# Sparse attention planned by beats: another order of the tiles, an earlier start of attending, and fewer filler products

## The reference, cut to what matters

```python
scores = indexer_scores(iqb, iwb, ik)                      # sum over 8 heads of w * relu(q_idx . k_idx)
scores = jnp.where((key_pos[None, :] <= qpos[:, None])[None], scores, -jnp.inf)
_, idx = lax.top_k(scores, n_sel)                          # n_sel = 256
valid = idx <= qpos[None, :, None]
return selected_attention(qb, gather_rows(k, idx), gather_rows(v, idx), valid)
```

## Time and profile before

| | us |
|---|---|
| median of three executions | 7112.57 |
| lowest and highest | 7103.77, 7126.53 |
| profiled execution, own time | 7120.96 |
| its span, first to last instruction | 7118.9 |

### The profile page before, as it was taken

The page is one execution under the profiler, slowest core; times in us unless marked ns, Lnnn a source line. Parts: engine busy times, 40 slices in busy tenths (PEclk is TensorE's granted clock), DMA queues, the critical chain, the costliest instruction groups (busy, mean ns, idle before and its releaser), DMA issues. The chain is left out here.

```text
span 7118.9 us, 108460 instructions
## 1 busy us (share of the span) xinstructions
PE 6246.8 (88%) x36876; PEld 3865.7 (54%) x36876; DVE 4227.9 (59%) x9694; ACT 4048.7 (57%) x5650; POOL 1652.2 (23%) x4028
## 2 busy tenths in 40 slices
PE   6999998878999999999999989797999599999960
PEld 2888886223454444444444455574555366767640
DVE  1555554478888888888888987553666510111027
ACT  1555554578898889999998888322333121222125
POOL 0111110222212322222332222001111133333335
PEclk9999998689999999999999999888999699999985
DMA  6121111000000000000000000332333388888888
GB/s 216 43 42 49 46 44 33 7 4 5 5 6 6 7 7 9 9 9 9 9 9 8 8 7 7 127 119 84 106 103 100 130 338 320 335 337 334 315 300 305
DMA packets 283509, 703.77 MB, mean 99 GB/s; under 512 B 105461, under 2 KB 151541, under 8 KB 242324
## 3 DMA queue, kind: packets, MB, share of 16 engines
q0 software_dynamic: 69408, 432.04, 16.3%
q1 hardware_dynamic: 210464, 252.99, 10.8%
q10 hardware_dynamic: 3190, 13.05, 0.5%
HBM read 559.38 MB, written 138.74 MB: 98 GB/s over the span
## 5 line engine op out<-in xcount | busy, mean ns | idle before, releaser
L1088 DVE TENSOR_SCALAR_CACHE_REDUCE at_junk<-at_key,at_thr 128x320 int8<-128x320 int16 (+44 forms) x990 | 1436.0, 1452 | 146.1 <-POOL at_thr L853 119.8
L887 ACT ACTIVATE at_junk<-at_key,at_thr 128x64 int8<-128x64 f32 (+47 forms) x627 | 1048.4, 1672 | 111.4 <-POOL at_thr L853 96.5
L1146 DVE CUSTOM_DVE_ANT_0 at_sm<-at_pS,at_drop 128x512 f32<-128x512 f32 (+3 forms) x1152 | 723.5, 642 | 176.8 <-PE at_pS L975 174.7
L975 PE MATMUL at_pS<-keep_KT,at_q 64*128 64x512 f32 (+3 forms) x2304 | 619.5, 615 | 82.5 <-DVE at_mx L1146 80.2
L1006 PEld LDWEIGHTS at_pT<-keep_ident,at_sm 128*128 128x128 f32 x4224 | 468.2, 144 | 410.2 <-issue 381.0
L986 PE MATMUL at_pD<-keep_IKT,at_iq 32*128 32x512 f32 (+3 forms) x2272 | 649.4, 649 | 17.9 <-ACT at_relu L911 17.0
L936 ACT ACTIVATE at_pt_sb<-at_pT 128x1024 f32<-128x1024 f32 (+2 forms) x576 | 548.8, 953 | 181.7 <-PE at_pT L1006 180.3
L911 ACT ACTIVATE at_relu<-at_pD 128x1024 f32<-128x1024 f32 (+3 forms) x568 | 542.2, 955 | 175.5 <-PE at_pD L986 172.9
L1006 PE MATMUL at_pT<-keep_ident,at_sm 128*128 128x128 f32 x4224 | 601.7, 285 | 4.7 <-DVE at_out L1175 2.2
L1017 PE MATMUL at_pO<-at_pt_sb,keep_V 128*64 128x128 f32 x8448 | 600.1, 283 | 0.7 <-DVE at_oT L1159 0.7
L2172 DVE TENSOR_TENSOR ex_gu<-ex_pg,ex_sg 128x256 f32<-128x256 f32 x98 | 41.6, 425 | 897.8 <-ACT ex_sg L2154 897.8
(11 more groups left out here) (443 smaller groups left out, 10376.7 us busy)
## 6 DMA issues: line engine op xcount, KB each, us to landing
scratch_ys<-ex_y SPq DMA_DIRECT2D x98, 512.0 KB, 2.6
scratch_x<-mx_x SPq DMA_DIRECT2D x33, 512.0 KB, 6.5
scratch_h<-mx_h SPq DMA_DIRECT2D x33, 512.0 KB, 2.6
cb_x<-scratch_x SPq DMA_DIRECT2D x33, 512.0 KB, 5.5
pj_x<-in_x_prompt SPq DMA_DIRECT2D x32, 512.0 KB, 3.3
mx_x<-in_x_prompt SPq DMA_DIRECT2D x32, 512.0 KB, 5.8
out_y_prompt<-cb_out SPq DMA_DIRECT2D x32, 512.0 KB, 4.5
scratch_qT<-pj_qT SPq DMA_DIRECT2D x33, 384.0 KB, 2.5
```

What stands on the lines that cost most here:

```text
L887: e.activation(junk[:, used(t, at.start, at.stop)], src[:, at], ACT.Sign, bias=bias, scale=-1.0, accum_out=cA[:, x:x + 1]).then_inc(sem("c ...
L975: last = e.matmul(pS[:, kv, 0:w], Q[rows, t % 4, p, :], KT[rows, c * CUT:c * CUT + w], start=True, stop=True)
L1088: e.tensor_scalar(junk[:, used(t, 0, N)], src[:, 0:N], value, None, ALU.is_ge, ALU.add, accum_out=cD[:, x:x + 1]).then_inc(sem("found", t), 1)
L1146: e.tensor_tensor_reduce(sm[:, kv, at:at + w], pS[:, kv, 0:w], drop[:, half(t), used(t, c * CUT, c * CUT + w)], -HD ** -0.5, -NEG, ALU.add ...
```

## The change

Five edits, all in the planner or on SyncE.

The order of the tiles: tile 15 takes the place of tile 3 as the first one searched, tile 27 comes after 28, and tiles 2 and 3 make the last step together. There are 20 steps instead of 21.

The start of attending: step k - 2, the one whose mask is made in the round, begins to be attended in that round, at beat 7 + 2B/5, and goes on until the next step opens. B takes three fifths of the units of step k - 3 and two fifths of those of step k - 2.

The fillers: a beat that holds a product with values gets none. SyncE loads queries one round earlier, and stores the last tile of a step at the end of the round instead of at the start of the next. The planner's code that shares counts between DVE and ACT is as it was and works on the new beats.

```diff
-        STEPS = [[0], [1], [3], [27], [31], [30], [29], [28], *([30 - x, x] for x in range(4, 15)), [15], [2]]
+        STEPS = [[0], [1], [15], [31], [30], [29], [28], [27], *([30 - x, x] for x in range(4, 15)), [2, 3]]
...
+        n_attend = lambda k: sum(G * CH(t) for t in STEPS[k]) if 0 <= k < NSTEP else 0
+        opens = []
         for k in range(2, NSTEP + 3):
             score = [(t, c) for t in group_of(k) for c in range(CH(t))]
-            attend = [(t, p, c) for t in (STEPS[k - 3] if 3 <= k else []) for p in range(G) for c in range(CH(t))]
-            n_score, n_attend = 4 * len(score), len(attend)
-            B = max(n_score, n_attend, 8)
+            n_score = 4 * len(score)
+            B = max(n_score, -(-(3 * n_attend(k - 3) + 2 * n_attend(k - 2)) // 5), 8)
...
+            opens.append(base + (7 + 2 * B // 5 if 0 < k - 2 < NSTEP else 0))
+            base += B
+        opens[-1] = max(base, opens[-2] + n_attend(NSTEP - 1))
+        for k in range(NSTEP):
+            attend = [(t, p, c) for t in STEPS[k] for p in range(G) for c in range(CH(t))]
             for i, (t, p, c) in enumerate(attend):
-                b = base + i * B // n_attend
+                b = opens[k] + i * (opens[k + 1] - opens[k]) // len(attend)
...
-            fills.append(int(max(0.0, FILL * max((v + a) / 2 + counts, 1.6 * len(shared)) - pe) / ARRAY))
+            fills.append(0 if beat.get("pv") else int(max(0.0, FILL * max((v + a) / 2 + counts, 1.6 * len(shared)) - pe) / ARRAY))
...
-                    for t in STEPS[k - 4][-1:] if k >= 4 else []:
+                    for t in STEPS[k - 3][:-1] if k >= 3 else []:
                         store(t)
                     for t in group_of(k + 1):
                         load_iq(t)
-                    if 0 < k - 2 < NSTEP:
-                        for t in STEPS[k - 2]:
+                    if k - 1 < NSTEP:
+                        for t in STEPS[k - 1]:
                             load_q(t)
-                    for t in STEPS[k - 3][:-1] if k >= 3 else []:
+                    for t in STEPS[k - 3][-1:] if k >= 3 else []:
                         store(t)
-                store(PT - 1)
```

More of the change, by code:

```diff
@@ L752, in phase_attend @@
                     due(turned + 3, "norm", (t, p))
-            base += B
         ahead = 0.0
```

## The result

The changed kernel takes 7195.16 us (median of four, 7174.05 to 7199.26), the kernel before 7112.75 (median of four). The ratio on record is 1.009, 95% interval 1.0068 to 1.0112; the two medians lie 1.2% apart and the two profiled spans 1.0%. It is slower by about 1%, where faster was forecast, and it lies outside the range. The profiled execution took 7193.93 us, its span is 7192.1 against 7118.9: 73 us more. Against the earlier trace rows the page shows the clock lower in five of its 40 slices (8, 13 to 15 and 24) and higher in one, and PE waiting more (the first line is the granted clock; then the logits after and before: times, busy us, mean ns, idle before).

What follows compares the result with a forecast made beforehand. PE was taken to set the pace most often in the steady stretch. Fillers 75 less clock 48, plus 14 beside it, made 41; with 7 for order, 48 us off 7121 gave 7073, median 7065; range 6955 to 7145.

Steps and rivals of the forecast that it cites:

- What bounds the kernel: Steady stretch of attention, 1856 us: PE, busy 94%, sets the pace most often; ACT waits 141 us for it.
- What the fillers are worth: Steady stretch: dropped fillers relieve PE of 150 us, of which half, 75 us, was taken as gain.
- The clock: Steady stretch: clock falls 0.04 to 0.94 without fillers, at 4.8 us a round, 48 us lost over ten rounds.
- Beside the steady stretch: Rounds 6 to 8 and 19 to 21: fillers dropped there bring about 14 us more gain.
- The order and earlier attending: All attention rounds, priced by like old rounds: 3284 us against 3291, a gain of 7 us.
- SyncE: Queries loaded a round earlier and last tiles stored earlier delay only loads needed some 90 us later: 0.
- the clock falls further: Rival: below about 0.92 in the steady stretch the clock costs more than fillers did; 7137 to 7192 us, chance 0.22.
- fillers free: Rival: fillers hide behind long ACT and DVE work and reordering is a wash; 0 to -15, 7105 us, chance 0.22.
- The signs: If right: fillers near 110 us; steady clock 0.92 to 0.97, ACT above 92%, its PE waits down a third, rounds 178 to 184 us.
- the sign of free fillers: ACT's waits for PE staying as long as now with fewer products in front of them.
- The range: Whole kernel's measured time, 6955 to 7145 us, taking in most of the free-fillers case and the mild part of the lower-clock case.

Runs made afterwards that it cites:

- e3: Kernel before with FILL 0.85 in place of 0.7 (360,851 filler columns instead of 171,646): 7249.11 us, 1.0184.
- e2: Changed kernel with the old rule for fillers, so new tile order and earlier attending only: 7127.01 us, 1.0004.
- e5: Kernel before with earlier attending and its loads and stores, tiles in the old order, fillers by the old rule: 7124.89 us, 1.0000.
- e1: Kernel before with only the filler edit, no fillers in beats with a product with values: 7206.02 us, 1.0118.
- e11: Changed kernel with the old filler rule, plus extra fillers in its first 48 beats (3072 columns in beat 2, then at least 256): 7140.01 us, 1.0026.
- e10: Kernel before, all filler columns kept, but those in beats with a product with values moved by 18 such beats, half a round: 7326.12 us, 1.0286.
- e6: Kernel before with FILL 0.6 in beats with a product with values, 56,621 of 121,173 columns staying: 7155.31 us, 1.0047.
- e12: Kernel before with extra fillers in its first 36 beats (3072 columns in beat 2, then at least 256): 7129.42 us, 1.0011.

## Why the prediction was wrong, point by point

*What bounds the kernel*: half right. With more fillers PE sets the pace of the whole stretch (e3), but ACT's waits for PE are not a store from which fillers can be paid back: they grew when the fillers went (141 to 161 us).

*What the fillers are worth*: mis-sized, 75 us predicted for ten rounds. Straight lines through rounds 11 to 18, time against granted clock, meet full clock at 184.0 us with fillers (before, e2, e5) and at 179.0 without (e1 and the changed kernel). That is 5 us a round, 50 in ten, as an estimate: it rests on lines drawn out to a clock that the rounds without fillers don't hold. The nearest to a direct reading is round 17, 187.2 us at 0.97 in the kernel before and 181.1 at 0.98 in e1: at nearly the same clock the round without fillers is the shorter one, so the loss comes through the clock. Whole executions give the same size. Over 63 of the kernel before, between 7098 and 7151 us, the time falls by 53 us for each 0.01 of an execution's mean clock. The four of e1 have a mean clock of 0.912 where these have 0.936, which by that line, drawn out as well, is some 130 us; e1 lost 82, so some 50 came back. (In the prediction's count, 121,553 is not what is left of 172,102 less 46,006, but what the old plan holds in beats with a product with values.)

*The clock*: the step that failed, twice over; the term of 48 us was too small. The fall was 0.06 by the stretches (0.98 to 0.92; 0.053 by the mean of the ten rounds' rows), not 0.04, and its price is 1.5 to 1.6 us a round for 0.01 (both lines, and e2 against e11), not 1.2. So 80 to 96 us instead of 48. With the worth of the fillers corrected too, 30 to 46 us lost, where the stretch shows 41 (changed kernel) and 42 (e1). These prices hold for fillers where the planner puts them: e10 and e6, forecast by them, took longer. The predicted 1.2 came from five rounds between 0.96 and 1.00, two of which differ by 9 us at the same clock; round 9 is not of their make, as it masks and attends single long tiles. Nor could the price be had safely from that trace: its rounds 11 to 18 give 1.6, and 1.0 without round 11.

The timeline of e1 shows one fall on PE, at the start of round 11. First the filler that the kernel before has in that beat, then e1 (start, us, product, idle before and its releaser), then e1's stretch behind the wait (columns as in the earlier trace rows):

```profile
2536.21 2.30 PE L1031 MATMUL at_pD<-keep_KT,keep_ident 128*128 128x512 f32 x6
2538.44 0.92 PE L986 MATMUL at_pD<-keep_IKT,at_iq 32*128 32x384 f32 x4
```

```profile
2572.11 1.13 PE L975 MATMUL at_pS<-keep_KT,at_q 64*128 64x512 f32 x4
2575.48 1.65 PE L986 MATMUL at_pD<-keep_IKT,at_iq 32*128 32x384 f32 x4 [2.24 <-ACT at_relu L911]
...
2579.84 2.08 PE L975 MATMUL at_pS<-keep_KT,at_q 64*128 64x512 f32 x4 [0.64 <-DVE at_mx L1146]
```
```profile
2575.50:2596.30 20.80, 19.00 (x75) 8.19 (x75) 12.38 (x28) 13.86 (x17) 5.42 (x22) 0.51 0.00 1
```

PE waits 2.24 us for a relu where a filler stood. The dot behind the wait takes 1.65 us instead of 0.92, and the logits 2.08 instead of 1.13. The clock stays at 0.51 for 21 us, in which PE is busy 19.0 us, ACT 13.9 and DVE 12.4: here the other two wait for slow products. In the kernel before the clock falls in these beats too, but for 7.5 us (0.55 from 2547.0 to 2554.5).

*Beside the steady stretch*: 14 us of gain were taken for rounds 6 to 8 and 19 on; against e2, which differs in the fillers only, these rounds are 12.5 and 3.6 us longer. The same sign error. By stages the missing fillers cost 37 us in the steady stretch, 16 here and 3 in rounds 2 to 5 against e2, and e2 is 8 us above the kernel before: together the 64 us of attention.

*The order and earlier attending*: right in that it is near nothing. 7 us gained were forecast; e2 measures 8 us lost in the profiled attention and 1.0004 in time, which can't be told from no change. The idle time at the end was moved, not removed. *SyncE*: 0 was forecast; it was not run by itself, but e2 and e5, which hold it, show no cost.

*The rivals*: "the clock falls further" is what happened, and the prediction named 0.92 as the point from which it decides. At exactly 0.92 the loss was already 41 us in the steady stretch, because that point was worked out from the two mis-sized prices. The Trainium skill, page "TensorE: Matmul & The Clock Gate", section "What's actually happening", gave this case: throttled is the default, activity releases it; the runs agree (0.98 with fillers, 0.92 without, 1.00 with more), and e10 adds that it matters where the activity lies (0.94 with the same columns). The other rule of the Trainium skill that I weighed, page "Perfetto Trace Analysis", section "Identifying the Most-Contended Engine", has weight-load busy time, beside the share of peak arithmetic, as the measure of TensorE's headroom. I took it to lead to "fillers free"; e3 speaks against that reading: there PEld is busy 50% of the steady stretch, little more than the 48% before, and the kernel is 1.84% slower with PE busy 98%.

*The signs*: the fillers' 124 us and the clock of 0.92 came near what was to show the forecast right; the rounds (187 to 195 us), ACT (89%) and its waits (up by 14%) did not. Waits of ACT that stay long with fewer products in front were named as the sign of free fillers. They came with slow products instead, so that sign can't tell the two apart; PE's own products, 94 us longer, can.

*The range* ended at 7145 and gave this case 0.22; the forecast leaned on a difference of two terms, each uncertain by more than the difference, and took a middle value for each.

## What to carry to other kernels

Price an operation that only holds the clock by both its terms, and read the clock's term from rounds with the same instructions at different clocks, before deciding on a difference between the two. Removing work from the engine that seems to pace only helps if the next thing it needs is ready; look at what it will wait for. A count of filler sized by the other engines' work in the same beat was near its best here in every direction tried (0.85, 0.6, none, only the large ones, moved): no run was faster than the kernel before, and e2, e5 and e12 can't be told from it.

## What the runs showed of the hardware that was not expected

The clock can fall while PE is far from idle: ahead of one fall PE was busy 5.79 of 8 us. And the same instructions can run with different falls: round 9 at 0.93 in e2 and 0.99 in e11, 9.3 us apart. Yet the falls are not loose chance: in rounds 12 to 22 the kernel before and e12, whose first rounds differ, agree in clock and within 0.1 us a round. Why one pattern comes rather than another is open.
